# A two-block network on one core: the joint of the blocks is computed in another order, and a gate row and two expert matrices are fetched at other places

## The chip, the core and the metric

The kernel runs on 1 core of one Trainium2 chip. The metric is the device time of one execution, in microseconds. In the profile PE is TensorE (with PEld its weight loads), DVE is VectorE, ACT is ScalarE, POOL is GpSimd, and SP is SyncE, which issues most of the transfers. A name such as SPq stands for that engine's own queue of instructions.

## The reference, cut to what matters

A sequence of 256 tokens of width 1024 goes through a first block (a gated linear recurrence, a feed-forward, a stick-breaking attention, a second feed-forward) and a final norm. Then a second block follows. Its norm, its eight projections, and its 32 experts with two chosen for each token are what the change touches:

```python
# end of the first block
h = h + swiglu_ffn(rms_norm(h, ffn_norm[1]), ffn_w_in[1], ffn_w_out[1])
x = rms_norm(h, final_norm)
# second block
mod = silu(c) @ w_ada + b_ada
sh1, sc1, g1, sh2, sc2, g2 = split(mod, 6)
h = rmsnorm(x, norm1_g) * (1.0 + sc1) + sh1
q_m, k_m, v_m, q_d, k_d, v_d, gate_m, gate_d = split(h @ w_in)
...                                   # two attentions, gates, output product
x = x + g1 * (merged @ w_out)
h2 = rmsnorm(x, norm2_g) * (1.0 + sc2) + sh2
y = hierarchical_moe(h2, ...)         # 32 experts: w_gate, w_up 1024x512, w_down 512x1024
x = x + g2 * y
return rmsnorm(x, final_g)
```

All is float32.

## The kernel before

**Layout.** Activations lie with their features on the partitions: `xT` and `hT` are 8 chunks (`k`) of 128 features x 256 tokens. Most products take float32 apart into a high and a low part (`PART_PAIRS`, three matmuls a pair): a weight unit is copied by ScalarE to the high part (`hi_unit`, L708) and subtracted by VectorE to the low part (`lo_unit`, L1077). Such a split product is 96 matmuls of 128x256 for a unit of 1024x512. A product without the split runs in full precision (`product_pair`, L1719).

**Stages.** Each engine has its own program, in a fixed order written out by hand, and they meet through semaphores. The order of weight units is `UNITS`; three places in a ring (`ring_a`) take them, and SyncE issues a load when the unit three places back has been used (`load_unit`, `wait_used`). The feed-forward has 11 steps of 256 columns in two slots (`ffn`, `gate_up`, `down`). Its sum stays in four banks of the accumulator memory, and the last step finishes them bank by bank, so that VectorE can add them to `xT` one after the other (`add_bank`, L1227). In the feed-forward norms, ScalarE and VectorE write the two parts of the gained, not yet normalised rows (`gained_high`, L790; `gained_low`, L1201), TensorE starts on these, and the root is multiplied in afterwards.

**The joint** between the blocks isn't built like that. After the last bank: squares on ScalarE (`norm_square`), sums with a matrix of ones on TensorE (`norm_sums`, L1692), root by Ln and Exp (`norm_root`, L679 and L680), scaling of `xT` on VectorE (`norm_scale`, L1052); then once more the same for the second norm, the shift (`norm_shift`, L685), qm's product in full precision, and from the same rows split in two the products of km, vm, qd, kd, vd and the gates. qm and km are rotated by a small product (`rotate`) and VectorE's arithmetic on its result. The modulation (`ada`, `gain`) is finished by VectorE in the joint, and POOL stores it to DRAM.

**The experts.** `wbuf` has three slots for an expert's gate, up and down matrices of 2048 KB each; the same memory holds the ring and the parts before. Expert 0's gate and up are issued after the last feed-forward step, its down and expert 2's gate after `pd`'s product, and the rest of experts 1 and 2 after the output product (`out0`, then `out1`). The routing then finds each expert's tokens, and `first_gu` marks expert 0's gate and up products. From here `load_next` refills a slot: gate and up when the expert's gate and up products are done, down when its down product is done. All these loads stand in order in SyncE's queue, behind its waits for `first_gu` (L582) and for the routing's first result (`info_ready`, L583). For each expert VectorE multiplies the output by `gate_tile`, a row of the modulation spread over the partitions, which POOL fetches from DRAM (L630) once the memory that it shares with `spread` is free. VectorE waits for that row and for `info_ready` ahead of `rest_of_window(0, 0, 0)`, the rest of expert 0:

```python
dve.wait_ge(spread_ev, 2)
dve.wait_ge(gate_in, 32)
dve.wait_ge(info_ready, 2)
n_more = dve.value_load(...)
...
rest_of_window(0, 0, 0)      # copies the transposed hidden rows (L1627); TensorE's down product (L2203) waits for it
```

## Time and profile before

| what | value |
|---|---|
| median of 3 runs | 1309.88 us (1301.74 to 1312.49) |
| profiled execution, own time | 1310.17 us |
| span from first to last instruction | 1308.3 us |
| TensorE busy | 1131.8 us (87%), weight loads 921.2 us (70%) |
| VectorE, ScalarE, GpSimd busy | 670.2, 414.5, 32.6 us |
| bytes moved | 362.47 MB, mean 277 GB/s |
| mean granted TensorE clock | 0.948 of full speed |

Busy times are shares of the whole span, while the stages have different limits. The slices of the page cut the span in 40 parts of 32.7 us. The chain of waits goes back from the last instruction, at each step to what released it.

### The profile page before, as it was taken

What the parts mean: (1) busy time and instruction counts of PE and PEld (TensorE: products, weight loads), DVE (VectorE), ACT (ScalarE), POOL (GpSimd) and SP (SyncE); (2) the same over time, 40 slices, a digit from 0 to 9 for tenths busy, and PEclk for the clock granted to TensorE, in tenths of its full rate; (3) what the DMA queues carried; (4) which work ended last, traced back from release to release, by engine and by line L of the source; (5) the groups of instructions that cost most, each with busy time, mean ns of one, the idle gap of its engine ahead of it and who ended that gap; (6) DMA issues with size and microseconds to landing.
All of it is one profiled execution on the core that took longest, in us unless ns stands there. A gap on an engine that the chain in (4) does not pass through costs nothing.

```text
span 1308.3 us, 23070 instructions
## 1 busy us (share of the span) xinstructions
PE 1131.8 (87%) x9324; PEld 921.2 (70%) x9325; DVE 670.2 (51%) x1040; ACT 414.5 (32%) x519; POOL 32.6 (2%) x71
## 2 busy tenths in 40 slices
PE   9999999999989999999899999778656667676666
PEld 8998999999868899999798899634223323332232
DVE  5799888886535565557256878542111122111113
ACT  3765333344474433335333673320000000000001
POOL 0000000000000000000100000000000000000000
PEclk9999999999999999999999999889888889888889
DMA  9577988855510965550945334689999999999996
GB/s 349 214 285 284 333 302 303 306 209 193 193 65 9 372 197 175 173 167 8 191 137 189 129 138 191 255 315 428 429 428 429 428 429 429 429 427 430 428 430 258
DMA packets 99400, 362.47 MB, mean 277 GB/s; under 512 B 4160, under 2 KB 51664, under 8 KB 84112
## 3 DMA queue, kind: packets, MB, share of 16 engines
q1 hardware_dynamic: 95216, 335.06, 67.2%
q0 software_dynamic: 3984, 26.50, 5.1%
q8 instruction: 43, 0.70, 0.2%
q10 hardware_dynamic: 144, 0.10, 0.0%
q14 instruction: 13, 0.11, 0.0%
HBM read 360.58 MB, written 1.06 MB: 276 GB/s over the span
## 4 chain that ended last, share of the span: by engine, by line
PE 59%; DMA 25%; DVE 9%; ACT 3%; issue 2%; SPq 1%; DVEq 0%; POOL 0%; POOLq 0%; ACTq 0%
DMA wbuf<-in_w_up 22%; PE ps L1843 16%; PE ps L1766 10%; PE ps L1729 8%; PE ps L2153 6%; PE ps L1750 3%; DVE parts L1077 3%; PE ps L2029 3%; PE ps L1775 2%; PE ps L1719 2%; PE ps L2203 2%; PE ps L2173 1%; DMA wbuf<-in_ffn_w_in 1%; PE ps L1926 1%; DMA wbuf<-in_lru_w_in 1%
## 5 line engine op out<-in xcount | busy, mean ns | idle before, releaser
L1843 PE MATMUL ps<-big_parts,parts 128*128 128x256 f32 x2112 | 259.6, 285 | 4.8 <-DVE parts L1077 3.7
L1843 PEld LDWEIGHTS ps<-big_parts,parts 128*128 128x128 f32 x2112 | 256.4, 191 | 6.0 <-DVE parts L1077 4.3
L2153 PE MATMUL ps<-wbuf,big 128*32 128x256 f32 x2176 | 166.9, 471 | 106.3 <-DMA wbuf<-in_w_up 103.0
L1077 DVE TENSOR_TENSOR parts<-wbuf,parts 128x2048 fp32r<-128x2048 f32 x90 | 204.4, 2287 | 89.4 <-ACT parts L822 45.2
L2153 PEld LDWEIGHTS ps<-wbuf,big 128*32 128x32 f32 x2176 | 92.9, 135 | 194.5 <-DMA wbuf<-in_w_up 84.4
L1639 DVE TENSOR_TENSOR big<-big,ps 128x128 f32<-128x128 f32 x33 | 9.5, 288 | 262.4 <-ACT big L1009 262.4
L1766 PE MATMUL ps<-big_parts,parts 128*128 128x256 f32 x1152 | 142.0, 283 | 1.7 <-DVE parts_f L1331 1.1
L1009 ACT ACTIVATE big<-ps 128x128 f32<-128x128 f32 x33 | 9.1, 277 | 421.9 <-PE ps L2153 421.9
L1766 PEld LDWEIGHTS ps<-big_parts,parts 128*128 128x128 f32 x1152 | 139.3, 189 | 2.1 <-issue 1.3
L1729 PE MATMUL ps<-parts_f,parts 128*128 128x256 f32 x720 | 103.0, 284 | 0.0
L1729 PEld LDWEIGHTS ps<-parts_f,parts 128*128 128x128 f32 x720 | 93.6, 192 | 0.1
L2203 PE MATMUL ps<-wbuf,big 128*32 128x512 f32 x544 | 67.1, 610 | 22.4 <-DVE big L1627 22.4
L1077 DVE TENSOR_TENSOR parts<-wbuf,parts_f 128x2048 fp32r<-128x2048 f32 x28 | 63.4, 2290 | 23.5 <-ACT parts_f L708 23.5
L2173 PE MATMUL ps<-big 64*128 64x512 f32 x272 | 67.9, 616 | 3.3 <-DVE big L1635 2.6
L727 ACT ACTIVATE parts<-wbuf 128x2048 fp32r<-128x2048 f32 x22 | 42.1, 1915 | 82.5 <-PE ps L1843 64.0
L822 ACT ACTIVATE parts<-wbuf 128x2048 fp32r<-128x2048 f32 x20 | 38.3, 1914 | 63.9 <-PE ps L1766 63.9
L1155 DVE SCALAR_TENSOR_TENSOR wbuf<-wbuf,big 128x1024 f32<-128x1024 f32 x48 | 56.0, 1221 | 0.3 <-DMA wbuf<-in_w_ada 0.3
L708 ACT ACTIVATE parts<-wbuf 128x2048 fp32r<-128x2048 f32 x24 | 44.7, 1906 | 34.7 <-PE ps L1729 18.3
L730 ACT ACTIVATE parts<-wbuf 128x2048 fp32r<-128x2048 f32 x22 | 42.2, 1917 | 41.4 <-PE ps L1843 37.5
L708 ACT ACTIVATE parts_f<-wbuf 128x2048 fp32r<-128x2048 f32 x28 | 52.4, 1903 | 3.4 <-PE ps L1729 3.3
L2203 PEld LDWEIGHTS ps<-wbuf,big 128*32 128x32 f32 x544 | 17.2, 110 | 47.2 <-issue 47.2
L2029 PE MATMUL ps<-parts_f 128*128 128x256 f32 x256 | 47.1, 286 | 1.3 <-DVE parts L1077 1.3
(334 smaller groups left out, 1388.2 us busy)
## 6 DMA issues: line engine op xcount, KB each, us to landing
wbuf<-in_w_down SPq DMA_DIRECT2D x32, 2048.0 KB, 38.0
wbuf<-in_w_gate SPq DMA_DIRECT2D x31, 2048.0 KB, 32.7
wbuf<-in_w_up SPq DMA_DIRECT2D x31, 2048.0 KB, 37.2
wbuf<-in_ffn_w_in SPq DMA_DIRECT2D x44, 1024.0 KB, 12.0
wbuf<-in_w_ada POOLq DMA_DIRECT2D x24, 1024.0 KB, 8.4
wbuf<-in_ffn_w_out SPq DMA_DIRECT2D x22, 1024.0 KB, 5.1
wbuf<-in_w_in SPq DMA_DIRECT2D x10, 2048.0 KB, 8.0
wbuf<-in_attn_w_qkv SPq DMA_DIRECT2D x6, 2048.0 KB, 8.6
```

Of the source, the lines that this page charges most:

```text
L708: nc.scalar.activation(halves(unit_parts(name)[0])[i], halves(unit_view(name))[i], ACT.Copy).then_inc(w_hi, 1)
L727: nc.scalar.activation(fg_part[0], ffn_views(slot)[0], ACT.Copy).then_inc(fg_hi, 1)
L730: nc.scalar.activation(fu_part[0], ffn_views(slot)[1], ACT.Copy).then_inc(fu_hi, 1)
L1077: nc.vector.tensor_tensor(lo, whole, hi.bitcast(F32), ALU.subtract).then_inc(done, 1)
L1155: ins = nc.vector.scalar_tensor_tensor(out=w, in0=w, scalar=1.0, in1=c_row, op0=ALU.mult, op1=ALU.mult, accum_out=ada[:, at:at + 1])
L1729: ins = mm(b[:, d * 256:(d + 1) * 256], w[pw][:, k, (m + d) * P:(m + d + 1) * P], rhs[px][:, k], start=(k == 0 and i == 0), stop=(k == kn ...
L1766: ins = mm(ps[:, 4 + f // 2, (f % 2) * 256:(f % 2 + 1) * 256], w[:, k, f * P:(f + 1) * P], r, start=(first and k == 0 and f % 2 == 0), sto ...
L1843: ins = mm(ps[:, b, d * 256:(d + 1) * 256], w[pw][:, k, d * P:(d + 1) * P], h_part_of[px][:, k], start=(k == 0 and d == 0 and i == 0), sto ...
L2029: ins = mm(ps[:, c % 2, d * 256:(d + 1) * 256], w[pw][:, k, m * P:(m + 1) * P], x_part[px][:, k], start=(k == 0 and i == 0), stop=(k == KC ...
L2153: ins = mm(at, rows, gu_place[s][:, :, k, r * P:(r + 1) * P], start=(k == 0), stop=(k == KC - 1))
L2173: ins = mm(ps[:, 4 + 2 * c + h, :], comb[q][rows, c * P:(c + 1) * P], yE[q][rows, :], start=False, stop=stop, skip_group_check=True)
L2203: ins = mm(ps[r * WIN:(r + 1) * WIN, 2, :], hidT[:, f * WIN:(f + 1) * WIN], d_place[s][:, f, h * 512:(h + 1) * 512], start=(i == 0), stop= ...
```

## The change

The joint is rewritten. qm's weights are split like the others, in the last feed-forward step, and vm's after the joint. qm's product is made in two halves from the gained rows with both norms' gains in one, with two more columns that hold the shift. The first norm's squares and the second norm's (with the final norm's gain) are both taken from the same `xT`, and the second mean is worked out from the first root. The joint root and the shift's product are put on qm afterwards; the other products take rows with root and shift in them. The same way of alternating sum and low part (`add_and_lower`) now serves the two feed-forward norms too, and the first weight split there stands behind it. The modulation's arithmetic moves ahead of the second feed-forward, its store to after that feed-forward's last load. POOL fetches the gate row after the routing weights are made (`route_sum`); `spread` and `zero_half` move to other memory for that, and VectorE waits for the products of `spread` before it clears the buffers now under it. SyncE issues expert 1's gate and expert 2's up after `out0`, and qd's load ahead of expert 0's gate and up.

Left out of the diff: renamed or merged semaphores, the tile list without qm0 and qm1, where qm's high part lies, and the order of the splits' counts.

```diff
+        x_shift_part = [big_parts[:, WORK + 2048 + i * 2064:WORK + 2048 + (i + 1) * 2064].rearrange("p (k t) -> p k t", k=KC) for i in range(2)]
+        x_rows_part = [v[:, :, 0:SEQ] for v in x_shift_part]
+        mean_5, root_5, root_45 = (flat(TMP + 512 + SEQ * i, SEQ) for i in range(3))
+        qm_bias = small[:, 392:396]
...
-        zero_half = big_half[:, 2 * 512:2 * 512 + 512]
+        zero_half = big_half[:, 2 * 1792:2 * 1792 + 512]
...
-        spread = flat(10752, 1024).rearrange("p (j t) -> p j t", j=2)
+        spread = flat(0, 1024).rearrange("p (j t) -> p j t", j=2)
...
             wait_used(sp, f"ffn1_{FFN_STEPS - 1}")
+            sp.dma_start(rope, a["rope"]).then_inc(rope_in, 16)
+            load_unit("qd")
             load_gate_up(sp, 0, 0)
-            sp.wait_ge(h_ready, 4 * KC)
-            sp.dma_start(rope, a["rope"]).then_inc(rope_in, 16)
-            for name in RING[RING.index("qd"):]:
+            for name in RING[RING.index("kd"):]:
                 load_unit(name)
 
             wait_used(sp, "pd")
             load_down(sp, 0, 0)
             load_gate_up(sp, 2, 2, (0,))
+            wait_used(sp, "out0")
+            load_gate_up(sp, 1, 1, (0,))
+            load_gate_up(sp, 2, 2, (1,))
             wait_used(sp, "out1")
-            load_gate_up(sp, 1, 1)
+            load_gate_up(sp, 1, 1, (1,))
             load_down(sp, 1, 1)
-            load_gate_up(sp, 2, 2, (1,))
             load_down(sp, 2, 2)
...
             pool.wait_ge(mod_ready, 2)
+            pool.wait_ge(fo_loaded[0], 16 * ffn_loads(1, FFN_STEPS - 1))
             for v, at in enumerate((gain[:, 1], ada[:, 24:32], ada[:, 40:48])):
...
             pool.dma_start(w_route, a["w_route"].rearrange("p (k n) -> p k n", k=KC)).then_inc(route_in, 16)
+            pool.wait_ge(route_sum, 1)
+            for h in range(2):
+                pool.dma_start(gate_tile[h * HALF_ROWS:(h + 1) * HALF_ROWS], mod_dram[2:3, h * 512:(h + 1) * 512].to_broadcast([HALF_ROWS, 512])).then_inc(gate_in, 16)
             pool.wait_ge(x_ready, 4 * 6)
             pool.dma_start(slot_no, a["slot_numbers"]).then_inc(slotno_in, 16)
-
-            pool.wait_ge(mod_stored, 48)
-            pool.wait_ge(spread_pe, 2)
-            for h in range(2):
-                pool.dma_start(gate_tile[h * HALF_ROWS:(h + 1) * HALF_ROWS], mod_dram[2:3, h * 512:(h + 1) * 512].to_broadcast([HALF_ROWS, 512])).then_inc(gate_in, 16)
...
                    if next_loads is None:
-                        hi_unit("vm" if layer else "q0")
+                        hi_unit("qm" if layer else "q0")
...
+            act.wait_ge(mod_ready, 2)
+            nc.scalar.activation(x_shift_part[0][:, :, SEQ:], ada[:, 0:KC].unsqueeze(2).to_broadcast([P, KC, 2]), ACT.Copy).then_inc(fh_hi, 1)
+            gained_high(4, x_rows_part[0], lambda k: gain[:, 0, k:k + 1])
+            for k in range(KC):
+                ins = nc.scalar.activation(squares[5][:, k], xT[:, k], ACT.Square, scale=col(R_FIN1 + k))
+                if k % 2 == 1:
+                    ins.then_inc(sq_done, 1)
             norm_root(4)
-            norm_square(5)
-            norm_root(5)
-            norm_shift(5, 0)
-            act.wait_ge(h_ready, 5 * KC)
-            for b in range(4):
-                nc.scalar.activation(x_part[0][:, 2 * b:2 * b + 2], hT[:, 2 * b:2 * b + 2], ACT.Copy).then_inc(fh_hi, 1)
-            copy_pair("qm0", qm[:, 0:2])
-            copy_pair("qm1", qm[:, 2:4])
+            act.wait_ge(sum_done, 6)
+            act.wait_ge(mean_ready, 1)
+            link(nc.scalar.activation(root_5, mean_5, ACT.Ln, bias=eps_col))
+            nc.scalar.activation(root_5, root_5, ACT.Exp, scale=-0.5).then_inc(root_done, 1)
+
+            def qm_shifted(h):
+                act.wait_ge(qm_scaled, h + 1)
+                for m in range(2 * h, 2 * h + 2):
+                    nc.scalar.activation(qm[:, m], qm[:, m], ACT.Identity, bias=qm_bias[:, m:m + 1]).then_inc(qm_kept, 1)
+
+            for k in range(KC):
+                act.wait_ge(h_part, k + 1)
+                nc.scalar.activation(x_part[0][:, k], hT[:, k], ACT.Identity, bias=ada[:, k:k + 1]).then_inc(fh_hi, 1)
+            qm_shifted(0)
+            qm_shifted(1)
+            hi_unit("vm")
             copy_pair("km0", km[:, 0:2])
             copy_pair("km1", km[:, 2:4])
             hi_unit("qd")
...
-            def scaled_low(layer, b):
-                gained_low(h_part_of, lambda k: col(R_FFN + KC * layer + k), fh_before[layer], b)
-
-            def add_squares(n):
+
+            def add_squares(n, banks=(1, 2, 3)):
 
                 into = squares[n][:, 0:2]
-                for b in range(1, 4):
+                for b in banks:
                     dve.wait_ge(sq_done, 4 * n + b + 1)
                     ins = nc.vector.tensor_tensor(into, into, squares[n][:, 2 * b:2 * b + 2], ALU.add)
                     if b < 3:
                         link(ins)
-                ins.then_inc(sq_added, 1)
-                nc.vector.nop().then_inc(h_ready, KC)
+                if banks[-1] == 3:
+                    ins.then_inc(sq_added, 1)
+                    nc.vector.nop().then_inc(h_ready, KC)
 
             def add_biased(b):
                 wait_bank(dve, "lo1", b)
                 ins = nc.vector.tensor_tensor(xT[:, 2 * b:2 * b + 2], ps[:, 4 + b, :].rearrange("p (k t) -> p k t", k=2), xT[:, 2 * b:2 * b + 2], ALU.add)
                 ins.then_inc(x_ready, 1)
 
...
-            def add_and_lower(last, ready, parts_of, gains, before):
+            def add_and_lower(add, n, parts_of, gains, before, early_squares):
 
                 for b in range(5):
+                    if b == 3 and early_squares:
+                        add_squares(n, (1,))
                     if b < 4:
-                        add_bank(last, b)
+                        add(b)
                     if b:
-                        dve.wait_ge(x_ready, ready + b)
+                        dve.wait_ge(x_ready, 4 * (n - 1) + b)
                         gained_low(parts_of, gains, before, b - 1)
-
+                add_squares(n, (2, 3) if early_squares else (1, 2, 3))
+
+            def ffn_gains(layer):
+                return lambda k: col(R_FFN + KC * layer + k)
+
+            add_and_lower(add_biased, 1, h_part_of, ffn_gains(0), fh_before[0], True)
+            split_u(0, 0)
             dve.wait_ge(silu_c, 1)
-            split_u(0, 0)
-            for b in range(4):
-                add_biased(b)
-                dve.wait_ge(x_ready, b + 1)
-                scaled_low(0, b)
-            add_squares(1)
             ada_unit(0)
             ada_unit(1)
 
                         split_u(1 - s, n + 1)
                         subtract(fd_part[1], ffn_views(s)[2], fd_part[0], fd_hi, n + 1, fd_lo)
                     else:
-                        lo_unit("vm" if layer else "q0")
+                        lo_unit("qm" if layer else "q0")
...
             o_copy(KC - 1)
             lo_unit("wo1")
             split_u(0, FFN_STEPS)
-            for b in range(4):
-                add_bank("wo1", b)
-                dve.wait_ge(x_ready, 4 * 2 + b + 1)
-                scaled_low(1, b)
-            add_squares(3)
-            dve.wait_ge(root_done, 4)
-            ffn(1)
-            add_residual(f"ffn1_{FFN_STEPS - 1}")
-
-
+            add_and_lower(lambda b: add_bank("wo1", b), 3, h_part_of, ffn_gains(1), fh_before[1], True)
             dve.wait_ge(ada_used, ADA_UNITS)
...
+            link(nc.vector.tensor_tensor(gain[:, 0], gain[:, 0], cols[:, R_FIN1:R_FIN1 + KC], ALU.mult))
...
-            norm_scale(4, lambda k: col(R_FIN1 + k), x_ready)
...
-            norm_scale(5, lambda k: gain[:, 0, k:k + 1])
-            for b in range(4):
-                subtract(x_part[1][:, 2 * b:2 * b + 2], hT[:, 2 * b:2 * b + 2], x_part[0][:, 2 * b:2 * b + 2], fh_hi, FH_LRU + 3 * KC + b + 1, fh_lo)
+            dve.wait_ge(root_done, 4)
+            ffn(1)
+
+            subtract(x_shift_part[1][:, :, SEQ:], ada[:, 0:KC].unsqueeze(2).to_broadcast([P, KC, 2]), x_shift_part[0][:, :, SEQ:], fh_hi, FH_QM + 1, fh_lo)
+            add_and_lower(lambda b: add_bank(f"ffn1_{FFN_STEPS - 1}", b), 4, x_rows_part, lambda k: gain[:, 0, k:k + 1], FH_QM + 1, False)
+            add_squares(5)
+            dve.wait_ge(root_done, 5)
+            dve.wait_ge(sum_done, 6)
+            link(nc.vector.scalar_tensor_tensor(out=mean_5, in0=ps[:, SUM_BANK[5], 0:SEQ], scalar=1.0 / D, in1=rstd[:], op0=ALU.mult, op1=ALU.mult))
+            nc.vector.tensor_tensor(mean_5, mean_5, rstd[:], ALU.mult).then_inc(mean_ready, 1)
+            dve.wait_ge(root_done, 6)
+            link(nc.vector.tensor_tensor(root_45, root_5, rstd[:], ALU.mult))
+
+            def shifted_low(k):
+                dve.wait_ge(fh_hi, FH_MOD + k + 1)
+                nc.vector.scalar_tensor_tensor(out=x_part[1][:, k], in0=hT[:, k], scalar=ada[:, k:k + 1], in1=x_part[0][:, k].bitcast(F32),
+                                               op0=ALU.add, op1=ALU.subtract).then_inc(fh_lo, 1)
+
+            for k in range(KC):
+                nc.vector.scalar_tensor_tensor(out=hT[:, k], in0=xT[:, k], scalar=gain[:, 0, k:k + 1], in1=root_45, op0=ALU.mult, op1=ALU.mult).then_inc(h_part, 1)
+                if k:
+                    shifted_low(k - 1)
+            shifted_low(KC - 1)
+            for h in range(2):
+                dve.wait_ge(qm_done, h + 1)
+                nc.vector.tensor_copy(qm_bias[:, 2 * h:2 * h + 2].unsqueeze(2), ps[:, 4 + 2 * h:6 + 2 * h, SEQ:SEQ + 1])
+                nc.vector.tensor_tensor(qm[:, 2 * h:2 * h + 2], ps[:, 4 + 2 * h:6 + 2 * h, 0:SEQ], root_45.unsqueeze(1).to_broadcast([P, 2, SEQ]), ALU.mult).then_inc(qm_scaled, 1)
+            for k in range(KC):
+                ins = nc.vector.scalar_tensor_tensor(out=xT[:, k], in0=xT[:, k], scalar=col(R_FIN1 + k), in1=rstd[:], op0=ALU.mult, op1=ALU.mult)
+                if k % 2 == 1:
+                    ins.then_inc(x_ready, 1)
+            lo_unit("vm")
 
             dve.wait_ge(rope_in, 16)
             for i, x in enumerate((qm, km, qd, kd)):
...
+            dve.wait_ge(spread_pe, 2)
             V.memset(yE[0], 0.0).then_inc(y_ev[0], 1)
             V.memset(comb[0], 0.0).then_inc(comb_ready[0], 1)
...
-            norm_sums(4)
-            norm_sums(5)
+            def qm_product(h):
+                w = unit_parts("qm")
+                for k in range(KC):
+                    if h == 0:
+                        pe.wait_ge(fh_lo, FH_QM + 1 + k + 1)
+                    for m in range(2 * h, 2 * h + 2):
+                        for i, (px, pw) in enumerate(PART_PAIRS):
+                            ins = mm(ps[:, 4 + m, 0:SEQ + 2], w[pw][:, k, m * P:(m + 1) * P], x_shift_part[px][:, k],
+                                     start=(k == 0 and i == 0), stop=(k == KC - 1 and i == 2))
+                ins.then_inc(qm_done, 1)
+
             def second_product(nm, h):
-                if nm == "qm":
-                    if h == 0:
-                        wait_unit(pe, nm)
-                    product_pair(f"{nm}{h}", unit_view(nm), 2 * h, KC, hT, 4 if h == 0 else None)
-                    return
                 if h == 0:
                     wait_parts(nm)
                 if nm[0] == "v":
             def rotate(nm, x, r):
 
                 for d in range(2):
-                    wait_evac(pe, f"{nm}{d}")
+                    if nm == "qm":
+                        pe.wait_ge(qm_kept, 2 * d + 2)
+                    else:
+                        wait_evac(pe, f"{nm}{d}")
...
-            for h in range(2):
-                second_product("qm", h)
-            pe.wait_ge(fh_lo, FH_LRU + 3 * KC + 4)
-            second_product("km", 0)
+            wait_parts("qm")
+            qm_product(0)
+            for n in (4, 5):
+                sums_added(n).then_inc(sum_done, 1)
+            qm_product(1)
+            wait_parts("km")
+            product_pair_rows("km0", unit_parts("km"), 0, KC, x_part, FH_MOD)
             rotate("qm", qm, 0)
             second_product("km", 1)
             second_product("vm", 0)
```

## Rows read from the trace of the kernel before

**Rows 1.** Page, parts 2 and 4: GB/s in 40 slices; the chain's shares.

```profile
GB/s 349 214 285 284 333 302 303 306 209 193 193 65 9 372 197 175 173 167 8 191 137 189 129 138 191 255 315 428 429 428 429 428 429 429 429 427 430 428 430 258
...
PE 59%; DMA 25%; DVE 9%; ACT 3%; issue 2%; SPq 1%; DVEq 0%; POOL 0%; POOLq 0%; ACTq 0%
```

**Rows 2.** Chain of waits, 612 to 660 us: start, us, engine, what, line, count.

```profile
619.88 3.47 PE ps L1692 x16
...
623.37 0.48 ACT rstd L679
...
625.92 5.23 PE ps L1692 x16
...
633.30 14.05 PE ps L1719 x64
647.36 5.75 PE ps L1729 x48
```

**Rows 3.** Timeline of the SyncE queue: start, us of issue, line, destination, source.

```profile
831.69 0.51 SPq L491 DMA_DIRECT2D wbuf<-in_w_down  x1
855.35 0.34 SPq L488 DMA_DIRECT2D wbuf<-in_w_gate  x1
...
873.11 0.33 SPq L491 DMA_DIRECT2D wbuf<-in_w_down  x1
```

**Rows 4.** Waits of the SyncE queue: us in total, times, longest.

```profile
SPq L583 <- DVE info L1610: 21.2, 1, 21.2
```

**Rows 5.** Windows of 1 us: busy us by engine, then PEclk, DMA share, GB/s.

```profile
626.00:627.00 1.00, 1.00 (x3) 0.82 (x4) 1.00 (x3) 0.81 (x2) 0.00 (x0) 0.50 1.23 349
...
870.00:871.00 1.00, 1.00 (x8) 0.23 (x4) 0.48 (x2) 0.00 (x0) 0.00 (x0) 0.50 0.16 66
```

**Rows 6.** Timelines of VectorE and TensorE around expert 0, 859 to 882 us.

```profile
859.77 0.23 DVE L1643 TENSOR_TENSOR cst<-rstd,ps 128x128 f32<-128x128 f32 x1
...
868.98 0.29 DVE L1627 COPY big<-ps 128x128 f32<-128x128 f32 x1 [8.99 <-issue]
...
862.36 0.33 PE L2196 MATMUL ps<-cst 128*128 128x128 f32 x1 [1.11 <-ACT big L994]
869.42 3.64 PE L2203 MATMUL ps<-wbuf,big 128*32 128x512 f32 x16 [6.73 <-DVE big L1627]
...
880.06 1.93 PE L2203 MATMUL ps<-wbuf,big 128*32 128x512 f32 x16 [0.47 <-DVE big L1627]
```

**Rows 7.** Transfers of the gate row: KB each, median us to landing.

```profile
big<-mod_dram POOLq DMA_DIRECT2D x2, 128.0 KB, 9.8
```

**Rows 8.** Timelines, 262 to 304 us and 600 to 662 us.

```profile
289.93 1.28 DVE L1227 TENSOR_TENSOR xT<-ps,xT 128x512 f32<-128x512 f32 x2
...
291.90 5.99 PE L1741 MATMUL ps<-parts_f,parts 128*128 128x256 f32 x48 [0.21 <-DVE parts_f L1201]
...
295.42 0.62 ACT L791 ACTIVATE big<-xT 128x512 f32<-128x512 f32 x1
...
613.72 4.49 DVE L1077 TENSOR_TENSOR parts<-wbuf,parts_f 128x2048 fp32r<-128x2048 f32 x2
...
618.12 2.49 DVE L1227 TENSOR_TENSOR xT<-ps,xT 128x512 f32<-128x512 f32 x4
...
632.13 3.25 DVE L1052 SCALAR_TENSOR_TENSOR big<-xT,gain,rstd 128x256 f32<-128x256 f32 x8 [3.77 <-ACT rstd L680]
632.65 3.30 ACT L685 ACTIVATE big<-big,ada 128x256 f32<-128x256 f32 x8 [0.55 <-DVE big L1052]
```

**Rows 9.** Chain of waits over the span: vm's product, 512 columns wide.

```profile
660.58 5.47 PE ps L1750 x24
```

**Rows 10.** Timeline, 84 to 134 us.

```profile
95.84 0.87 DVE L1221 SCALAR_TENSOR_TENSOR xT<-ps,cols,xT 128x256 f32<-128x256 f32 x2
...
104.30 0.88 DVE L1201 SCALAR_TENSOR_TENSOR big_parts<-xT,cols,big_parts 128x256 fp32r<-128x256 f32 x2 [0.65 <-ACT big_parts L790]
...
114.67 11.66 PE L1843 MATMUL ps<-big_parts,parts 128*128 128x256 f32 x96 [0.50 <-DVE parts L1077]
```

More of the change, by code:

```diff
@@ L192, in program @@
         square_0 = wbuf[:, 2 * MATRIX + KC * SEQ:3 * MATRIX].rearrange("p (k t) -> p k t", k=KC)
-        squares = [square_0, hT, hT, fm(WORK), hT, hT]
+        squares = [square_0, hT, hT, fm(WORK), hT, fm(WORK)]
         rg = wbuf[:, 2 * MATRIX:2 * MATRIX + KC * SEQ].rearrange("p (k t) -> p k t", k=KC)
@@ L362, in unit_parts @@
             k, lo = 4 if name[0] in "plow" else KC, (parts_0, parts_1, parts_2)[RING.index(name) % PLACES]
-            if name in SPLIT_2:
+            if name == "qm":
+                hi = parts[:, UNIT:2 * UNIT]
+            elif name in SPLIT_2:
                 at = HI_AT[SPLIT_2.index(name) % 2]
@@ L433, in wait_used @@
                 eng.wait_ge(ada_used, ADA_UNITS)
+            elif name == "qm":
+                eng.wait_ge(qm_done, 2)
             elif name in SUMMED:
@@ L680, in norm_root @@
                 nc.scalar.activation(rstd[:], rstd[:], ACT.Exp, scale=-0.5).then_inc(root_done, 1)
-            def norm_shift(n, shift):
-                for k in range(KC):
-                    act.wait_ge(h_part, k + 1)
-                    nc.scalar.activation(hT[:, k], hT[:, k], ACT.Identity, bias=ada[:, shift + k:shift + k + 1]).then_inc(h_ready, 1)
             def copy_pair(name, dst, func=ACT.Copy, scale=1.0):
@@ L944, in _ @@
             act.wait_ge(av_evac, 8)
-            nc.scalar.activation(fm(0, 4), qd, ACT.Square).then_inc(osq_done, 1)
+            nc.scalar.activation(fm(0, 4), qd, ACT.Square).then_inc(sq_done, 1)
             act.add_instruction(mybir.InstLoadActFuncSet(name=nc.get_next_instruction_name(), act_func_set_id=EXP_LN_TABLE, ins=[], outs=[]))
             hi_half("pd", 1)
-            act.wait_ge(osum_done, 1)
+            act.wait_ge(sum_done, 7)
             sums = fm(0, 4).rearrange("p k t -> p (k t)")
             link(nc.scalar.activation(sums, ps[:, 4:6, :].rearrange("p b n -> p (b n)"), ACT.Ln, scale=1.0 / P, bias=eps_col))
-            nc.scalar.activation(sums, sums, ACT.Exp, scale=-0.5).then_inc(oroot_done, 1)
+            nc.scalar.activation(sums, sums, ACT.Exp, scale=-0.5).then_inc(root_done, 1)
             for i in range(2):
@@ L1365, in _ @@
                 ins.then_inc(mod_ready, 1)
-            norm_scale(5, lambda k: gain[:, 0, k:k + 1])
-            for b in range(4):
-                subtract(x_part[1][:, 2 * b:2 * b + 2], hT[:, 2 * b:2 * b + 2], x_part[0][:, 2 * b:2 * b + 2], fh_hi, FH_LRU + 3 * KC + b + 1, fh_lo)
+            dve.wait_ge(root_done, 4)
+            ffn(1)
+            subtract(x_shift_part[1][:, :, SEQ:], ada[:, 0:KC].unsqueeze(2).to_broadcast([P, KC, 2]), x_shift_part[0][:, :, SEQ:], fh_hi, FH_QM + 1, fh_lo)
```

46 lines of the change are left out of this document (22 added, 24 removed).

## The prediction, made before the changed kernel was run

> **What bounds the kernel now.** I read the page's slices first [rows 1]. They show two kernels in one. Up to slice 27 the transfers move less than 380 GB/s, and most of the chain runs through TensorE (59%); from slice 28, 883 us, to the last but one they move 427 to 430 GB/s without a break. That second part is the expert stage, where 2048 KB matrices are fetched one behind the other; one of 2.097 MB takes 4.9 us at 429 GB/s. So the end of the kernel is the moment from which that stream is unbroken, plus a constant. A microsecond counts if it brings that moment forward: any microsecond of the chain ahead of it does, one inside the stream does not.
>
> The chain from 619.88 shows the joint [rows 2]: sums of squares, a gap, sums again, a gap, the full-precision qm product (14.05 us), and only at 647.36 km. That is 27.5 us, of which 4.7 are gaps.
>
> The SyncE queue shows where the stream starts [rows 3]. Five matrices are issued between 829.5 and 831.7 and take 5 x 4.9 = 24.5 us from 830.5, thus to 855. Expert 3's gate follows at 855.35, and its down matrix only at 873.11. The longest late wait of that queue is 21.2 us for the routing's first result, from 832.2 to 853.4 [rows 4]. In the microsecond from 870 the transfers carry 66 GB/s at a share of 0.16 [rows 5]: they have run dry, and they stay so until about 1.1 us after 873.11, thus 874.2. From there the stream is unbroken.
>
> Why 873.11: this issue waits for expert 0's down product, which runs 869.42 to 873.06. Its transpose was done at 862.69; then VectorE, idle since 860.00, copies it only at 868.98 [rows 6]. VectorE waits for the gate row, which POOL issues at 856.7 and 857.2 and which takes a median 9.8 us to land [rows 7], thus 867. The remaining 2 us are its loads of registers, done behind that wait.
>
> **The change, part by part.** The sum is made against the profiled execution, 1310.17 us (span 1308.3, 1.9 around it); the median of the three runs, 1309.88, is 0.3 lower.
>
> *Joint.* The new order starts qm's product from gained, unnormalised rows, and puts the root on afterwards. The same pattern stands at the end of the first feed-forward [rows 8]: VectorE's first residual sum at 289.93, the product of 48 split matmuls from 291.90 (1.97 later) for 5.99 us, ScalarE's last square done at 296.04 (6.11 later), the sums of two squares 0.9 us (a quarter of the 3.47 in [rows 2]). VectorE is free for the residual at 618.12 in the joint, behind a weight split; that stays, since qm's split takes vm's place, of the same size. With 0.2 for the two shift columns I get: first half of qm 620.3 to 626.3; ScalarE's squares to 624.4, then its eight new ones at 0.41 each (the shifts' duration) to 627.7; VectorE's last sum 0.8 later, 628.5; TensorE's second sum to 629.5; second half of qm 5.75, to 635.25. km follows at once if its rows are there. They come by root, mean, second root, joint root, one scale and one shift: two VectorE operations on 256 columns at 0.45, two activations 0.95 (0.48 the first, [rows 2]), then 0.4, 0.4, 0.5 and 0.45, so the first row is ready at 633.2 and the last 7 x 0.85 later, at 639.2. km reads its last row at 635.25 + 7 x 0.72 = 640.3. TensorE bounds it. km starts at 635.25 in place of 647.36: **12.1 us** less.
>
> Behind km, qm's scaling and shifts end at 641.7 and its rotation starts at 641.0 on the first half, without a stall. VectorE then scales xT (3.25 us) and splits vm (two halves of 2.25 [rows 8]) to 648.65, as ScalarE's half must end first, at 645.4. vm's product wants it at 641.0 + 1.9 + 5.75 = 648.65. This has no slack: 0 taken, 2 us as the upper bound. qd's load is now issued at 635.25, before expert 0's gate and up, and is wanted at 661; kd's stands behind 14.7 us of transfers and lands near 657, wanted at 661.9 by ScalarE. The ring behind is released by TensorE's products, so it moves along, and the 12.1 us last to the routing. I take 12.0.
>
> Three prices aren't in the trace. (a) A product 258 columns wide: 256 cost 0.120 us each (5.75/48 [rows 2]), 512 cost 0.228 (5.47/24 [rows 9]), full precision 0.439 (14.05/32). I take 0.120, the nearest width; the ends are no cost and +10.4 us for 96 at 0.228. (b) The clock. After the gap of 2.57 us it is granted at 0.50 (1.2 GHz) at 626 [rows 5], and 16 sums take 5.23 instead of 3.47; after the gap of 2.15 it is not lowered. The new joint has gaps of 0.4 and 1.0 us around a short sum, nearer to the second case: I take 0, with 1.8 as the bound. (c) The two shift columns' split, 0.2; neither end matters beyond 0.1.
>
> *First feed-forward.* VectorE now adds and lowers in alternation, with the 2.2 us weight split behind it, not ahead. Before, its first add is at 95.84 and its last lowering ends at 105.18 [rows 10], in steps of 2.31, each waiting for ScalarE. Now adding starts at 93.7, paced by TensorE's banks every 1.95, and lowering ends near 101.9. Squares, split, the two modulation units and the gate's split follow in the same lengths; TensorE's step of 114.67 starts at 113.3. **1.3 us**; bounds 0 and 2.5. At the second layer the same code buys nothing: there the gate product already runs without a stall, and two waits for weights follow. The modulation arithmetic moved to that place, some 2 us, lies in VectorE's wait for the root.
>
> *Gate row early.* POOL issues it after the routing weights are made, near 794 by the old times, beside out1's load, which lands at 800 and is read at 808: even delayed by 3 us it is covered. Then VectorE's register loads follow at 860.0, it is idle at 861.1, copies the transpose at 862.75, and the down product runs from 863.15. TensorE is idle for 0.5 instead of 6.7 us, keeps its full clock and needs 1.93, as at 880.06, not 3.64 [rows 6]. The down matrix of expert 3 is issued at 865.2 instead of 873.11: **7.9 us**. The added wait for the spread products (done at 856.2) stands ahead of memsets at 858.8: free.
>
> By the Trainium skill (DMA: Bandwidth & Descriptors, Queues, rings and completion order) each engine takes turns between queues, packet by packet. By that rule a row on POOL's queue would not have waited behind SyncE's megabytes, and this part would give nothing. The 9.8 us of [rows 7] speak against it, whichever of queue or source is slow.
>
> *Expert 1's gate and expert 2's up early.* They are issued at 818, when the queue runs empty, and land by 830 in idle time. That leaves three matrices at 829.9, done at 845.2. Then nothing can be issued until 855.35: the wait of [rows 4] does not move against the routing. The transfers idle 11 us just where the two matrices lay before. Expert 3's gate and up run 856.45 to 866.25; the down matrix, issued at 865.2, joins at 866.3, 7.9 before 874.2. Without the early loads the same two would end at 865 and the down matrix still start at 866.3. So I cost this part at **0**.
>
> Sum: 12.0 + 1.3 + 7.9 = 21.2; 1310.17 - 21.2 = **1289.0 us**.
>
> **The rivals.** *The early loads pay in full*, 9.8 more: 1279. For it, the stream bounds the end; against it, the 21.2 us wait. 0.08.
> *The gate row pays nothing*, because the next wait (the gather, ScalarE's last rows, a register load) holds the down product: 1297. Against it, the transpose ready at 862.69. 0.12.
> *The joint gives 10 back*: the 258-column products cost as 512, or ScalarE's and VectorE's added work delays vm and the rotations by that much: 1299. 0.08.
> *Nothing arrives*: the time comes back at the ring's loads, 1310. 0.05.
> *Slower*: the odd width makes the split products run like full precision, 96 x (0.439 - 0.120) = 30.6 more: 1319.6. It decides from 0.34 us a matmul. The nearest row, 512 wide, speaks against it. 0.04. The skill's FP8 and Floating Point Precision (TensorE Precision Notes) gives true FP32 four passes; 0.439 against 0.120 is 3.7, so rows agree.
>
> **How the numbers follow.** The forecast has 0.63, with its bounds (1.8, 2 and 1.3 up, 1.2 down, and 3 for the scatter of a median) from 1284 to 1296. About 1%, 13 us, is what can be told from no change, thus below 1296.8. Faster: 0.63 + 0.08 + half of the rival at 1297 = 0.77. Same: 0.06 + 0.08 + 0.05 = 0.19. Slower: 0.04. The range takes in the rivals at 1279, 1297 and 1299: 1279 to 1301.
>
> **What would show it.** Right: km's first matmul 15 to 16 us after the last ffn1 bank, no 5 us sum block; VectorE's copy within 0.2 us of the transpose near expert 0; transfers idle for about 11 us ahead of expert 3's gate. Wrong: idle time ahead of vm, qm matmuls above 0.13 us, full transfers between the third matrix and expert 3's gate, or another wait ahead of the first down product.

## The result, and the profile after

The changed kernel takes 1289.54 us, the median of four runs (1289.05 to 1292.79); the kernel before, run beside it, 1308.08 (1301.74 to 1312.49). The ratio is 0.9869, with a 95% interval of 0.9835 to 0.9902: 17 us faster by the ratio (13 to 22), 18.5 by the medians, where the sum of the forecast was 21.2. The profiled execution took 1292.79 (span 1291.0), the longest of the four and 3.3 above their median, so its trace holds some 3 us that the others don't have.

The joint first, from the changed kernel's timeline of TensorE between 612 and 650 us (start, duration, line, shapes, count, and in brackets the idle time ahead with what ended it):

```profile
617.13 5.99 PE L2007 MATMUL ps<-big_parts,parts 128*128 128x258 f32 x48 [0.30 <-DVE big_parts L1221]
623.44 1.13 PE L1735 MATMUL ps<-big,cst 128*128 128x256 f32 x4 [0.33 <-DVE big L1230]
625.50 1.13 PE L1735 MATMUL ps<-big,cst 128*128 128x256 f32 x4 [0.92 <-DVE big L1230]
```

and its chain of waits from there on:

```profile
626.62 5.75 PE ps L2007 x48
632.37 5.75 PE ps L1778 x48
638.12 1.73 PE ps L2028 x8
639.85 5.75 PE ps L1766 x48
645.60 4.56 PE ps L1787 x20
```

These lines answer to [rows 2]. The two blocks of 16 sums are gone, two short sums stand between the halves of qm's product, and km starts at 632.37 in place of 647.36. A product 258 columns wide costs 5.75/48 = 0.120 us a matmul, as one of 256. Nothing stands idle ahead of the second km half or of vm.

The first feed-forward's step answers to [rows 10], 114.67 then:

```profile
113.40 11.65 PE L1880 MATMUL ps<-big_parts,parts 128*128 128x256 f32 x96 [1.43 <-DVE parts L1097]
```

The SyncE queue, which answers to [rows 3]:

```profile
806.03 11.47 SPq L497 DMA_DIRECT2D wbuf<-in_w_up  x2
817.55 0.91 SPq L500 DMA_DIRECT2D wbuf<-in_w_down  x2
843.00 0.34 SPq L497 DMA_DIRECT2D wbuf<-in_w_gate  x1
843.45 1.75 SPq L497 DMA_DIRECT2D wbuf<-in_w_up  x1
852.80 0.33 SPq L500 DMA_DIRECT2D wbuf<-in_w_down  x1
859.55 0.33 SPq L497 DMA_DIRECT2D wbuf<-in_w_gate  x1
859.97 0.38 SPq L497 DMA_DIRECT2D wbuf<-in_w_up  x1
863.97 0.33 SPq L500 DMA_DIRECT2D wbuf<-in_w_down  x1
875.89 0.33 SPq L497 DMA_DIRECT2D wbuf<-in_w_gate  x1
```

Expert 3's gate is issued 12.35 us earlier than in [rows 3], its down matrix 20.31 earlier. Windows of 2 us show what lies around them (busy time and count of PE, PEld, DVE, ACT, POOL, then the granted clock, the DMA share and GB/s):

```profile
836.00:838.00 2.00, 2.00 (x14) 1.88 (x13) 1.86 (x8) 0.54 (x2) 0.00 (x0) 0.82 0.00 0
838.00:840.00 2.00, 1.91 (x37) 0.89 (x40) 1.86 (x11) 2.00 (x6) 0.00 (x0) 1.00 0.00 0
840.00:842.00 2.00, 2.00 (x37) 0.69 (x34) 1.79 (x8) 1.24 (x4) 0.00 (x0) 1.00 0.00 0
...
860.00:862.00 2.00, 1.52 (x8) 0.37 (x6) 0.45 (x3) 0.00 (x0) 0.00 (x0) 1.00 0.81 254
```

The transfers stand still just ahead of expert 3's gate, as the early loads were expected to leave them. And around expert 0 and the next two, from the timelines of VectorE and TensorE, where [rows 6] stood:

```profile
850.38 0.29 DVE L1664 COPY big<-ps 128x128 f32<-128x128 f32 x1 [2.74 <-PE ps L2243]
...
850.02 0.33 PE L2243 MATMUL ps<-cst 128*128 128x128 f32 x1 [1.11 <-ACT big L1014]
850.82 1.92 PE L2250 MATMUL ps<-wbuf,big 128*32 128x512 f32 x16 [0.48 <-DVE big L1664]
853.21 3.23 PE L2200 MATMUL ps<-wbuf,big 128*32 128x256 f32 x56 [0.47 <-POOL big L662]
858.71 0.64 PE L2200 MATMUL ps<-wbuf,big 128*32 128x256 f32 x8 [2.26 <-issue]
862.00 1.92 PE L2250 MATMUL ps<-wbuf,big 128*32 128x512 f32 x16 [0.48 <-DVE big L1664]
869.90 5.79 PE L2200 MATMUL ps<-wbuf,big 128*32 128x256 f32 x64 [5.98 <-issue]
```

The copy follows its transpose at once and the down product runs at full clock: the wait for the row is gone. But two stops are new, 2.26 us within expert 1's gate and up product and 5.98 ahead of expert 2's. No semaphore ends them ("issue"), and behind the second the granted clock is 0.50, so that the product takes 5.79 instead of 3.66 us. They show in the queue above: expert 5's gate is issued 16.3 us behind expert 4's, where it was 8.6 in before (877.61 and 886.24). The window at 860 shows the stream short of work. How much of the time at the end this costs is another question, taken up below: in this stage the transfers set the time, and a stop costs nothing as long as they go on beside it (experiment 4 shows one).

One more difference belongs to neither kernel. TensorE's first product of the second output projection takes 8.62 us here instead of 5.99, for it runs at half clock (1.2 GHz) behind an idle time of 2.71 us that the kernel before has as well, without the drop:

```profile
780.00:782.00 2.00, 2.00 (x12) 2.00 (x11) 2.00 (x3) 0.61 (x1) 0.14 (x1) 0.50 0.99 397
```

### The profile page after: what moved, and what is told of

It reads as the page before. It is cut to its first block, busy times and chain, and to the rows that moved or that the text cites. A ratio compares the mean times of both kernels' runs of the same rounds, so it can differ in the third digit from the quotient of the medians.

```text
span 1291.0 us, 23141 instructions
## 1 busy us (share of the span) xinstructions
PE 1120.0 (87%) x9332; PEld 907.3 (70%) x9333; DVE 685.0 (53%) x1069; ACT 420.7 (33%) x532; POOL 32.7 (3%) x71
## 4 chain that ended last, share of the span: by engine, by line
PE 58%; DMA 24%; DVE 11%; ACT 3%; issue 3%; SPq 1%; POOLq 0%; DVEq 0%; POOL 0%; ACTq 0%
DMA wbuf<-in_w_up 22%; PE ps L1880 16%; PE ps L1803 9%; PE ps L1766 8%; PE ps L2200 6%; DVE parts L1097 3%; PE ps L1787 3%; PE ps L2076 3%; PE ps L1812 2%; PE ps L2220 1%; PE ps L2250 1%; DMA wbuf<-in_ffn_w_in 1%; PE ps L1756 1%; PE ps L1963 1%; DVE wbuf L1175 1%
## 5 line engine op out<-in xcount | busy, mean ns | idle before, releaser
L1097 DVE TENSOR_TENSOR parts<-wbuf,parts 128x2048 fp32r<-128x2048 f32 x92 | 208.8, 2287 | 88.6 <-ACT parts L829 45.2
L2200 PEld LDWEIGHTS ps<-wbuf,big 128*32 128x32 f32 x2176 | 83.6, 133 | 206.9 <-issue 105.3
L1766 PE MATMUL ps<-parts_f,parts 128*128 128x256 f32 x704 | 98.4, 284 | 0.0
L1766 PEld LDWEIGHTS ps<-parts_f,parts 128*128 128x128 f32 x704 | 90.5, 192 | 0.1
L734 ACT ACTIVATE parts<-wbuf 128x2048 fp32r<-128x2048 f32 x22 | 42.1, 1916 | 83.6 <-PE ps L1880 60.0
L715 ACT ACTIVATE parts<-wbuf 128x2048 fp32r<-128x2048 f32 x26 | 48.4, 1905 | 33.1 <-PE ps L1766 18.1
L829 ACT ACTIVATE parts<-wbuf 128x2048 fp32r<-128x2048 f32 x20 | 38.3, 1913 | 63.9 <-PE ps L1803 63.9
L737 ACT ACTIVATE parts<-wbuf 128x2048 fp32r<-128x2048 f32 x22 | 42.2, 1916 | 40.5 <-PE ps L1880 36.6
L2220 PEld LDWEIGHTS ps<-big 64*128 64x128 f32 x272 | 23.4, 186 | 34.1 <-issue 32.4
```

What stands on the lines that cost most here:

```text
L715: nc.scalar.activation(halves(unit_parts(name)[0])[i], halves(unit_view(name))[i], ACT.Copy).then_inc(w_hi, 1)
L734: nc.scalar.activation(fg_part[0], ffn_views(slot)[0], ACT.Copy).then_inc(fg_hi, 1)
L737: nc.scalar.activation(fu_part[0], ffn_views(slot)[1], ACT.Copy).then_inc(fu_hi, 1)
L1097: nc.vector.tensor_tensor(lo, whole, hi.bitcast(F32), ALU.subtract).then_inc(done, 1)
L1766: ins = mm(b[:, d * 256:(d + 1) * 256], w[pw][:, k, (m + d) * P:(m + d + 1) * P], rhs[px][:, k], start=(k == 0 and i == 0), stop=(k == kn ...
L2200: ins = mm(at, rows, gu_place[s][:, :, k, r * P:(r + 1) * P], start=(k == 0), stop=(k == KC - 1))
```

## The experiments

"Changed" is the changed kernel, "before" the kernel before. Each ratio is against before on the same chip. To compare two parts I multiply the difference of ratios by 1309 us.

**1. Changed, without the early loads.**

```
-            wait_used(sp, "out0")
-            load_gate_up(sp, 1, 1, (0,))
-            load_gate_up(sp, 2, 2, (1,))
             wait_used(sp, "out1")
-            load_gate_up(sp, 1, 1, (1,))
+            load_gate_up(sp, 1, 1)
             load_down(sp, 1, 1)
+            load_gate_up(sp, 2, 2, (1,))
             load_down(sp, 2, 2)
```

> The changed kernel with its matrix loads in the old order: expert 1's gate and expert 2's up matrix are issued behind the output product's second half again, nothing else differs. Theory (early loads pay nothing, because expert 3's gate load waits for the routing and not for transfers): 1289.5 us as the changed kernel, within 1.5; expert 3's gate is issued at about 843 us as before, and the 9 us in which transfers stood idle ahead of it are filled. Rival (the two early loads brought about the 9.8 us of idle transfers forward): 1299 us, expert 3's gate or the first down products later by up to that.

Measured: 1292.5 us (before 1309.15), ratio 0.9872 [0.984, 0.9904]; changed has 0.9869. Expert 3's gate is issued at 842.29, and the window before it is full of transfers:

```profile
836.00:842.00 6.00, 5.80 (x74) 2.92 (x75) 5.45 (x26) 4.04 (x9) 0.00 (x0) 1.00 1.00 423
```

By the medians this is 3.0 us above changed, outside the 1.5 that were expected; by the ratios it is 0.4, and the interval is some 4 us wide to either side, so a small worth of the loads can't be excluded here. The rival at 1299 is out: the slowest run took 1296.12. The loads fill idle time and leave as much idle time behind.

**2. Changed, with the gate row late.**

```
-            pool.wait_ge(route_sum, 1)
-            for h in range(2):
-                pool.dma_start(gate_tile[h * HALF_ROWS:(h + 1) * HALF_ROWS], mod_dram[2:3, h * 512:(h + 1) * 512].to_broadcast([HALF_ROWS, 512])).then_inc(gate_in, 16)
             pool.wait_ge(x_ready, 4 * 6)
             pool.dma_start(slot_no, a["slot_numbers"]).then_inc(slotno_in, 16)
+            pool.wait_ge(spread_pe, 2)
+            for h in range(2):
+                pool.dma_start(gate_tile[h * HALF_ROWS:(h + 1) * HALF_ROWS], mod_dram[2:3, h * 512:(h + 1) * 512].to_broadcast([HALF_ROWS, 512])).then_inc(gate_in, 16)
```

> The changed kernel with the gate row issued late again, behind the second matrix product of the routing's spread, buffers as in the changed kernel. Theory (the early gate row is worth 7.9 us): 1297.4 us; DVE's copy for expert 0 waits for the row, the first down product starts about 8 us later, expert 3's down load is issued near 861 instead of 852.8 us. Rival (the row's early load pays nothing since the stream of expert matrices is full anyway): 1289.5 us.

Measured: 1293.89 us, ratio 0.9886 [0.9855, 0.9917]: 4.4 us more than changed by the medians, 2 by the ratios. The wait is back and the stop ahead of expert 2's product has gone, as its timeline of TensorE shows:

```profile
853.51 3.64 PE L2250 MATMUL ps<-wbuf,big 128*32 128x512 f32 x16 [6.33 <-DVE big L1664]
864.50 1.93 PE L2250 MATMUL ps<-wbuf,big 128*32 128x512 f32 x16 [0.48 <-DVE big L1664]
866.74 3.66 PE L2200 MATMUL ps<-wbuf,big 128*32 128x256 f32 x64 [0.31 <-issue]
```

A stop within expert 3's product stays (2.42 us, at 881.28; 2.12 in changed). Expert 3's down load comes 17.36 us behind its gate (839.84 to 857.20), against 9.80 in changed. At this place the row is worth 7.6 us, at the end less.

**3. Before, with the gate row early alone.**

```
-        zero_half = big_half[:, 2 * 512:2 * 512 + 512]
+        zero_half = big_half[:, 2 * 1792:2 * 1792 + 512]
-        spread = flat(10752, 1024).rearrange("p (j t) -> p j t", j=2)
+        spread = flat(0, 1024).rearrange("p (j t) -> p j t", j=2)
...
+            dve.wait_ge(spread_pe, 2)
             V.memset(yE[0], 0.0).then_inc(y_ev[0], 1)
```

POOL's lines are those of experiment 2 the other way round, and its wait for `mod_stored` is dropped with them.

> The kernel before with the gate row issued early, and the buffers and the one wait that this needs, nothing else changed. Theory: 7.9 us less than the kernel before, 1300.2 us; expert 3's down load issued 8 us earlier than at 873.1 us. Rival (row pays nothing): 1308.1 us. Rival (it pays only together with the early loads): between 1305 and 1308 us.

Measured: 1304.32 us, ratio 0.9961 [0.9943, 0.998]: 5.1 us (2.6 to 7.5), not 7.9. The stop is there with the row, in a kernel that has nothing else of the change:

```profile
865.61 1.92 PE L2202 MATMUL ps<-wbuf,big 128*32 128x512 f32 x16 [0.47 <-DVE big L1626]
...
883.25 5.34 PE L2152 MATMUL ps<-wbuf,big 128*32 128x256 f32 x62 [4.07 <-issue]
```

**4. Before, with the early loads alone** (the lines of experiment 1 the other way round).

> The kernel before with expert 1's gate and expert 2's up matrix loaded while the output product's second half runs, nothing else changed. Theory (early loads pay nothing): 1308.1 us as the kernel before, transfers idle for some 9 us ahead of expert 3's gate at 855.4 us. Rival: 9.8 us less, 1298.3 us.

Measured: 1307.25 us, ratio 0.9998 [0.9977, 1.0018]. Its trace has the hole, 5 GB/s over the 6 us from 846 (expert 3's gate at 851.34):

```profile
846.00:852.00 6.00, 5.90 (x71) 2.38 (x71) 5.52 (x28) 4.32 (x10) 0.00 (x0) 1.00 0.02 5
```

No gain is resolved in either kernel (here at most 3.0 us, by the interval). The same trace has the stop within expert 2's product, although the row is late:

```profile
881.54 5.33 PE L2155 MATMUL ps<-wbuf,big 128*32 128x256 f32 x62 [4.89 <-issue]
```

So the early row isn't what the stop needs, though before and experiments 2 and 5, with the row late too, don't have it. And it costs no transfer here: in windows of 1 us from 876 to 882 they go on at 393 to 459 GB/s.

**5. Changed, with row and loads both as before**, so that the joint and the first order are left (the edits of 1 and 2).

> The changed kernel with both the gate row and the two matrix loads as before: only the rebuilt joint and the order ahead of the first feed-forward are left of the change. Theory of the prediction (12.0 + 1.3 for these): 1308.1 - 13.3 = 1294.8 us. Theory as the row's own runs have changed it (the row is worth about 4.5 us at the end, not 7.9, because PE's unexplained stops in the first experts come into the open): the changed kernel's 1289.5 + 4.5 = 1294 us. Rival (row and loads are worth 7.9 only together): 1297.4 us. The two matrix loads give a stretch without transfers in both, so the row late without them should equal the row late with them, 1293.9 us.

Measured: 1298.45 us (before 1309.43), ratio 0.991 [0.9892, 0.9927]: 11.8 us (9.6 to 14.1), where 13.3 were forecast. From here to experiment 1, which differs by the row alone, it is 0.0038 or 5.0 us: the row's price a second time. 11.8 + 5.1 = 16.9, and the whole change has 17.1, so the parts add up. By its median it lies nearest the rival at 1297.4, by which row and loads are worth 7.9 only together; experiments 3 and 1 speak against that, for there the row is worth 5 without the loads. I had expected 1294 in its place; the medians put it 4.6 us above experiment 2, from which only the loads should part it. The intervals of the two ratios overlap, and experiments 1 and 4 give the loads no value, so I leave that difference open.

**6. Changed, with the old order ahead of the first feed-forward** (wait, weight split, add and lower in turn, squares).

> The changed kernel with the order ahead of the first feed-forward as before: VectorE waits for the silu of the condition and lowers an up matrix first, then adds and lowers bank by bank, then the squares. Theory: 1.3 us more than the changed kernel, 1290.8 us, the first feed-forward's second step starting at 114.7 instead of 113.4. Rival (the time is taken up in a wait further on): 1289.5 us.

Measured: 1292.42 us, ratio 0.9871 [0.9853, 0.9889], 0.0002 above changed (by the medians 2.9 us, where 1.3 were forecast): at the end it can't be told from nothing. Its trace has the step:

```profile
114.99 10.23 PE L1884 MATMUL ps<-big_parts,parts 128*128 128x256 f32 x84 [0.57 <-DVE parts L1097]
```

1.6 us later than 113.40, and the load of the attention's weights at 300 us is still 1.4 later (300.63 against 299.23). So the part is real up to there, and its worth at the end isn't resolved.

**7. Changed, with the two sums behind the second half of qm.**

```
             qm_product(0)
-            for n in (4, 5):
-                sums_added(n).then_inc(sum_done, 1)
             qm_product(1)
+            for n in (4, 5):
+                sums_added(n).then_inc(sum_done, 1)
```

> The changed kernel with TensorE's two sums of squares (1.13 us each) behind the second half of the first query product instead of between its halves. Theory (the second half covers VectorE's and ScalarE's work from the sums to the first lowered input, 626.6 to 630.7, and 1.7 us are left over at 632.4): without that cover the first key product starts 4.1 us later, at 636.5, and the whole takes 1293.6 us. Rival (the key product waits for its split weights or the stream absorbs it): 1289.5 us, within 1.

Measured: 1295.53 us, ratio 0.9897 [0.9882, 0.9912], 3.7 us above changed by the ratios and 6.0 by the medians, where 4.1 were forecast. TensorE's timeline and a window behind it:

```profile
615.95 11.77 PE L2007 MATMUL ps<-big_parts,parts 128*128 128x258 f32 x96 [0.30 <-DVE big_parts L1221]
633.69 0.68 PE L1778 MATMUL ps<-parts_f 128*128 128x256 f32 x2 [4.25 <-DVE parts_f L1388]
```

```profile
634.00:636.00 2.00, 2.00 (x11) 2.00 (x11) 2.00 (x6) 1.44 (x3) 0.00 (x0) 0.50 1.14 454
```

The stop is 4.25 us, as forecast from the spans of the other engines. km starts 17.74 us after qm instead of 15.24, only 2.5 later, as the short waits of 0.33 and 0.92 ahead of the sums have gone. The rest came through the clock, at 0.50 behind the stop: the first half of km takes 7.50 us instead of 5.75 in the chain, 1.75 more. Together this is 4.25, close to the forecast's 4.1. So the second half of qm is what hides the roots.

**8. Changed, with the stream held**: no load from expert 3 on until expert 2's down product is done.

```
             sp.wait_ge(info_ready, 1)
+            sp.wait_ge(down_done[0], 3)
```

> The changed kernel with SyncE's loads from expert 3 on held until expert 2's down product is done, so that TensorE goes through experts 0 to 2 with no matrix transfers beside it. Theory (the stops of 2.3 and 6.0 us ahead of and within the gate and up products of experts 1 and 2, which no semaphore ends, come from instructions that land late behind full transfers): they fall below 1 us, and experts 1 and 2 follow each other within some 9 us each; the kernel as a whole takes some 20 us more. Rival (the stops belong to entering the loop, whatever the transfers do): they stay at 2 and 6 us.

Measured: 1319.55 us, one run. TensorE's timeline:

```profile
853.85 3.99 PE L2201 MATMUL ps<-wbuf,big 128*32 128x256 f32 x64 [0.53 <-POOL big L663]
860.50 1.92 PE L2251 MATMUL ps<-wbuf,big 128*32 128x512 f32 x16 [0.47 <-DVE big L1665]
865.08 3.66 PE L2201 MATMUL ps<-wbuf,big 128*32 128x256 f32 x64 [2.66 <-issue]
```

With no transfers beside it, the stop within expert 1's product is gone, and the one ahead of expert 2's is 2.66, not below 1. In the seven traces of changed and its variants with the early row and the transfers running (changed, 1, 6, 7, 9, 10, 11) the first is 0.54 to 2.26 us long and the second 4.67 to 5.98. As far as one run can show it, both theories hold a part: some 2.7 us belong to getting there, and 2 to 3 more, with the first stop, to the transfers. The whole took 30 us more, not the 20 forecast. That it is instructions which land late is supported by the packets of the queue named "instruction" in changed: none in the 3 us from 864, one in the 3 us in whose last tenth TensorE starts again. That is an argument, not a proof.

**9 to 11. Changed once more, and two small moves.**

> The changed kernel itself once more, beside the next two on the same chip: 1289.5 us within 2. In its trace TensorE's first product of the second output projection either shows half clock for about 2 us (as six of the traces so far) or for 5.5 us (as the first trace of the changed kernel).

Measured: 1289.53 us (before 1307.54), ratio 0.9875 [0.9853, 0.9896]. Its trace (span 1286.4) has no half clock in the projection at all. That is neither of the two forms that were expected, but a third:

```profile
780.00:782.00 2.00, 2.00 (x19) 2.00 (x18) 2.00 (x2) 0.00 (x0) 0.00 (x0) 1.00 1.01 412
```

Experiment 10 waits for the second piece of routing information ahead of expert 3's gate (info_ready 2 for 1 in SyncE's wait).

> The changed kernel with SyncE's load of expert 3's gate released by the second piece of routing information instead of the first, so about 3.4 us later (846.4 instead of 843.0 us). Theory (from that load on the time is the stream's: issue of this load, plus bytes, plus the stretches in which nothing moves): the whole takes as much longer, 1292.9 us. Rival (TensorE's pace in the first experts sets it, since the stream waits for slots there anyway): 1289.5 us.

Measured: 1291.17 us, ratio 0.9882 [0.9861, 0.9902]. The edit moved the load less than I thought: its down load follows it by 8.91 us instead of 9.80, so it came 0.9 later, not 3.4. Against experiment 9 on the same chip the ratios give 0.9 us more and the medians 1.6, too little to tell the theories apart. Inconclusive.

Experiment 11 puts the gate row behind `pool.wait_ge(x_ready, 4 * 6)`.

> The changed kernel with the gate row issued when the output product has been added (near 817 us) instead of at 779 us, still 29 us ahead of its use. Theory (only its being there at expert 0 counts): 1289.5 us, DVE's copy for expert 0 still directly behind the transpose. Rival (the row's issue beside the output matrix's load slowed TensorE's next product): 1 to 2.6 us less, no half clock there.

Measured: 1291.17 us, ratio 0.9875 [0.9854, 0.9897], the same as experiment 9 by the ratio and 1.6 us above it by the medians. The long half clock at the projection was there although the row came only at 816.50, so the row isn't its cause; experiments 2 and 5, without an early row, show the shorter form of it.

## Why the prediction was right, and where not

The forecast was 1289.0 us, the measurement 1289.5. The direction, the parts that pay and the part that does not are as forecast. The near-exact sum owes something to luck: it was made against an execution 2 us above the median of before, and one term was too large by some 3 us. The gain was forecast at 21.2 and measured at 17 to 18.5.

- *Joint, 12.0.* km starts 14.99 us earlier, at a joint that starts 3.06 earlier: 11.9. The sequence was as forecast (second sum ends 626.6, km directly behind the second half). The three open prices: 258 columns cost as 256, the clock stayed full, and vm, foreseen without slack, has no idle time. Joint and first order together measure 11.8 at the end (9.6 to 14.1, experiment 5), where 13.3 were forecast.
- *First feed-forward, 1.3.* 1.3 by the traces' own times, 1.6 by experiment 6; up to 300 us. At the end not resolved.
- *Gate row, 7.9: the term that was mis-sized.* Expert 3's down load comes 20.31 us earlier, of which 12.35 are its gate load's shift, so 7.96. (The other pairs of traces with the row late and early give 7.6, 8.4 and 9.4: the wait was read rightly, its tenth is luck.) The step that failed is the one from this shift to the end. The sum let expert 3's gate and up matrices "run 856.45 to 866.25", so that nothing would move until 874.2 and a down matrix 7.9 earlier would gain 7.9. Windows of 1 us in before show transfers (these two, and the row's 0.26 MB) for 3 us longer, until 869.4:

```profile
868.00:869.00 1.00, 0.00 (x0) 0.00 (x0) 0.02 (x1) 0.00 (x0) 0.00 (x0) 0.50 1.00 426
869.00:870.00 1.00, 0.58 (x4) 0.23 (x8) 1.00 (x3) 0.00 (x0) 0.00 (x0) 0.50 0.43 180
...
871.00:872.00 1.00, 1.00 (x11) 0.28 (x7) 0.00 (x0) 0.00 (x0) 0.00 (x0) 0.50 0.00 0
872.00:873.00 1.00, 1.00 (x12) 0.38 (x8) 0.00 (x0) 0.00 (x0) 0.00 (x0) 0.50 0.06 16
873.00:874.00 1.00, 1.00 (x16) 0.49 (x11) 0.69 (x1) 0.00 (x0) 0.00 (x0) 0.50 0.00 0
```

In the 5 us from 869 the transfers fell 4.4 us short of what 430 GB/s would have moved; that, and not 7.9, stood there to be gained, with some 2 us that were lost ahead of it at 254 to 393 GB/s. The traces can be added up so, over the 99 us that start 1.1 behind the issue of expert 3's gate, in us short of 430 GB/s:

| traces | to 1.1 behind the down matrix's issue | from there on | sum |
|---|---|---|---|
| row late (before, 2, 4, 5) | 6.0 to 7.5, mean 6.8 | 1.2 to 2.1, mean 1.7 | 7.1 to 9.5, mean 8.5 |
| row early (changed, 1, 3, 6, 7, 9, 10, 11) | 0.8 to 1.5, mean 1.0 | 1.5 to 5.2, mean 2.7 | 2.7 to 6.1, mean 3.7 |

The difference of the sums, 4.8 us, is the row's worth at the end; the timings say 5.1 and 5.0. Of the 3.1 missing from 7.9, some 2 were never there, because the stream was moving in that time, and 1.0 comes back later. Whether this 1.0 is the stops' price isn't shown. In changed (3.7 in that column) and experiment 11 (5.2) the stream is short beside them. But experiments 1 and 3 have the stops and 1.5 and 1.9 there, no more than the kernels with the row late, and experiment 4 has a stop of 4.89 and 1.2. Why the stops arise stays open too (experiment 8). The rival at this place, another wait ahead of the first down product, is out: nothing but the copy stands ahead of it.
- *By the Trainium skill (DMA: Bandwidth & Descriptors, Queues, rings and completion order)* each DMA engine takes turns between queues, packet by packet; by that rule a late row would not have waited, and this part was to give nothing. It gave 5. Rows do not show the row being let past: 8.3 to 10.4 us to land late (before, 2, 4, 5), and 6.1 to 8.6 early, 6.7 of them at 779 us in changed, where the output matrix was being loaded. Whether the queue or the source is slow, no run here separates.
- *Early loads, 0.* Right as far as resolved: ratio 0.9998 alone, 0.4 us by the ratios when taken out. The stretch without transfers was 9 us, not 11.
- *What would show it.* km's first matmul came 15.5 us after the last ffn1 bank (its product runs 610.90 to 616.8), no 5 us sum block, the copy directly behind the transpose, the idle stretch: all there. Of the signs against none came; the stops lie behind the first down product, a place that the list did not name.

## What to carry to other kernels

A load moved into idle time pays only if the next issue of its queue waits for the queue; if it waits for data, the idle time moves behind the load. When a wait ahead of a transfer is removed, the gain is the time in which the transfers stood still, not the time by which the issue comes earlier: here 5 us of 7.9, and windows of 1 us in the trace of before showed it. Look behind the wait as well, at code that runs for the first time: here stops of 2 to 6 us, which no semaphore explains, lay there, and what they cost depended on whether the stream ran short beside them. And unnormalised products with the root put on afterwards hide a whole chain of small operations, provided that a piece of the same product is kept back to cover it.

## What the runs showed that I had not expected

The clock behind one and the same idle time of TensorE is not fixed. Behind 2.7 us ahead of the second output projection's first product it stayed full (before, 4, 9), was at 0.50 for some 3.4 us (1, 2, 3, 5, 6, 7, 8, 10) or for some 6.8 us (changed, 11), by the granted clock in windows of 2 us. From the output matrix's first issue to that of expert 0's down matrix it is 30.6 us, 31.9 to 32.1 or 33.2 to 33.3: 0, 1.4 or 2.7 us of time. The same happens at 368 us, behind 2.46 us in before and 2.47 in changed. The windows from 370 show it, before first:

```profile
370.00:372.00 2.00, 2.00 (x11) 1.58 (x11) 0.59 (x1) 0.81 (x1) 0.00 (x0) 0.50 0.00 0
```

```profile
370.00:372.00 2.00, 2.00 (x14) 1.46 (x12) 0.00 (x0) 1.86 (x3) 0.00 (x0) 1.00 0.00 0
```

From there to TensorE's next long product (399.60 and 396.78) changed gained 1.6 us that no part of the change brought: experiment 4, which is before's code up to this place, was granted the full clock there too, and experiment 10, which is changed's, 0.50 from 368 to 370. Two traces can differ by some 3 us through this alone, so a term of that size is to be read from stretches between such places, as the joint's 11.9 was.
